# The recurrence of the last mixer: levels walked upwards in place, by products of gates

## What is computed

```python
f = lb + (1.0 - lb) * sigmoid(f_logit)
k = 1.0 - f
S_t = diag(f_t) S_(t-1) + k_t i_t^T          # 128 x 128 per head
o_t = S_t^T (q_t * 128 ** -0.5)
o = o * rsqrt(mean(o * o) + eps) * norm_g * silu(gate)
```

## Time and profile before

| | us |
|---|---|
| median of three executions | 3402.69 |
| the profiled execution | 3395.66 |
| its span, first to last instruction | 3393.8 |
| TensorE busy in the span | 3285.3 |
| recurrence, from 2340 to 2437 | 97 |

### The profile page before, as it was taken

How to read it: one execution, slowest core, us unless ns; L and a number is a source line. 1 busy time by engine, 2 the same in 40 slices (tenths; PEclk the granted TensorE clock), 3 DMA queues, 4 the chain that set the end, 5 groups by cost and what they waited for, 6 DMA issues and landing times.

```text
span 3393.8 us, 48243 instructions
## 1 busy us (share of the span) xinstructions
PE 3285.3 (97%) x16266; PEld 2647.4 (78%) x16266; DVE 1973.4 (58%) x2513; ACT 1761.5 (52%) x2142; POOL 1335.6 (39%) x670
## 2 busy tenths in 40 slices
PE   8999999999999999999999999998899999999997
PEld 6888887778888788888778888787666788888884
DVE  4335684653354433551563333457766799999998
ACT  5552334545523555322545533414662688888884
POOL 3444442144444444444134444343202344444441
PEclk9999999999999999999999999899999999999998
DMA  3225331022243222433422233222102899999997
GB/s 125 97 95 168 117 102 50 20 88 98 98 160 130 82 99 93 158 127 118 131 75 94 98 95 104 68 97 93 38 8 73 324 384 384 388 387 390 381 370 294
DMA packets 128099, 534.40 MB, mean 157 GB/s; under 512 B 24464, under 2 KB 24720, under 8 KB 100112
## 3 DMA queue, kind: packets, MB, share of 16 engines
q1 hardware_dynamic: 107136, 499.63, 41.5%
q0 software_dynamic: 20736, 33.60, 2.6%
q10 hardware_dynamic: 144, 0.08, 0.0%
HBM read 531.64 MB, written 41.94 MB: 169 GB/s over the span
## 4 chain that ended last, share of the span: by engine, by line
PE 60%; issue 25%; POOL 8%; DVE 5%; ACT 2%; DMA 1%; POOLq 0%; DVEq 0%; SPq 0%; ACTq 0%
PE ps L827 17%; PE ps L829 16%; PE ps L828 16%; POOL w_lo L1927 8%; PE ps L1308 2%; PE ps L989 1%; PE ps L1014 1%; PE ps L999 1%; PE ps L1373 1%; PE ps L847 1%; PE ps L1060 1%; PE ps L1129 1%; PE ps L1093 1%; PE ps L1292 0%; PE ps L1327 0%
## 5 line engine op out<-in xcount | busy, mean ns | idle before, releaser
L1927 POOL TENSOR_TENSOR w_lo<-stage_buf,w_hi 128x1024 fp32r<-128x1024 f32 (+1 forms) x396 | 968.9, 2447 | 1508.6 <-ACT w_hi L1471 1508.6
L1471 ACT ACTIVATE w_hi<-stage_buf 128x1024 fp32r<-128x1024 f32 (+1 forms) x396 | 414.0, 1046 | 1186.9 <-PE ps L829 1126.1
L827 PE MATMUL ps<-x_hi,w_hi 128*128 128x512 f32 x1984 | 776.1, 391 | 7.3 <-POOL w_lo L1927 5.6
L828 PE MATMUL ps<-x_lo,w_hi 128*128 128x512 f32 x1984 | 774.7, 390 | 0.0
L829 PE MATMUL ps<-x_hi,w_lo 128*128 128x512 f32 x1984 | 774.5, 390 | 0.0
L827 PE MATMUL ps<-hid,w_hi 128*128 128x512 f32 x1312 | 518.8, 395 | 2.6 <-issue 1.7
L829 PE MATMUL ps<-hid,w_lo 128*128 128x512 f32 x1312 | 511.6, 390 | 0.0
L828 PE MATMUL ps<-hid,w_hi 128*128 128x512 f32 x1312 | 510.8, 389 | 0.0
L827 PEld LDWEIGHTS ps<-x_hi,w_hi 128*128 128x128 f32 x1984 | 374.2, 189 | 89.3 <-POOL w_lo L1927 7.5
L829 PEld LDWEIGHTS ps<-x_hi,w_lo 128*128 128x128 f32 x1984 | 374.0, 189 | 77.6
L828 PEld LDWEIGHTS ps<-x_lo,w_hi 128*128 128x128 f32 x1984 | 374.2, 189 | 77.3
(11 more groups left out here) (405 smaller groups left out, 4952.8 us busy)
## 6 DMA issues: line engine op xcount, KB each, us to landing
stage_buf<-in_gu SPq DMA_DIRECT2D x176, 512.0 KB, 3.3
big<-in_exp_gu SPq DMA_DIRECT2D x72, 1024.0 KB
h_buf<-in_exp_gu SPq DMA_DIRECT2D x72, 1024.0 KB
s_buf<-in_exp_dn SPq DMA_DIRECT2D x72, 1024.0 KB
stage_buf<-in_down SPq DMA_DIRECT2D x64, 512.0 KB, 3.6
stage_buf<-in_down SPq DMA_DIRECT2D x32, 384.0 KB, 3.2
sil_buf<-in_ada SPq DMA_DIRECT2D x24, 512.0 KB, 4.3
tmp_buf<-in_ada SPq DMA_DIRECT2D x24, 512.0 KB, 4.2
```

The lines of the kernel that those rows point to most:

```text
L827: nc.tensor.matmul(o, a_hi, b_hi, start=start, stop=False)
L828: nc.tensor.matmul(o, a_hi, b_lo, start=False, stop=False)
L1471: nc.scalar.activation(w_hi[s][:, 0:n], stage[s][:, 0:n], ACT.Copy).then_inc(upper_done, 1)
L1927: nc.gpsimd.tensor_tensor(w_lo[s][:, 0:n], stage[s][:, 0:n], w_hi[s][:, 0:n].bitcast(F32), ALU.subtract).then_inc(parted, 1)
```

## The change

The tree is walked upwards, from neighbours to halves of a block, and no logarithm is taken. `hgrn_decays` multiplies neighbouring gates once, pairs of those again, and so on, which gives the decay of each run of 2, 4, ... 128 tokens (`hg_decay`). Query and key tiles (`hg_qw`, `hg_kw`) hold all four heads and are updated in place: before level r, whose halves are `1 << (r - 1)` wide, they are what its scores need; after it the queries of the second halves are multiplied with the decay of the first half and the keys of the first halves with that of the second (one factor, repeated over the run). Level 0 is the diagonal, with the raw queries. Heads are done in pairs: step i is level `i % 16 // 2` of head `i // 16 * 2 + i % 2`. Levels 6 and 7 compute only the pieces they need. What crosses blocks uses the same tiles once more: `near` (next block), one more update of one block, and `far`; ScalarE makes these copies now. Head sums and the rows of heads 2 and 3 are placed later, partly inside `gated`. The diff, cut, eight columns of indentation taken off:

```diff
-hg_b = [rstd[:, :]] + [xn_buf[:, (4 + hd) * T:(5 + hd) * T] for hd in range(1, 4)]
-hg_e = [tmp[:, 0, :], tmp[:, 1, :], s_buf[:, 5 * T:6 * T], s_buf[:, 6 * T:7 * T]]
-hg_kl, hg_ql = ([s_buf[:, (j + s) * T:(j + s + 1) * T] for s in range(2)] for j in (0, 2))
+hg_qw, hg_kw = tiles(s_buf[:, 0:4 * T], T), tiles(pt_buf[:, 0:4 * T], T)
+hg_scores = [tiles(s_buf[:, (4 + hd) * T:(5 + hd) * T], P) for hd in range(4)]
+hg_decay = [big[:, R_HF:R_HG], tmp_buf[:, :]] + [sil_buf[:, 1024 - (1024 >> n):1024 - (512 >> n)] for n in range(6)]
+hg_far = [xn_buf[:, 768 * j:768 * j + 768] for j in range(2)]
...
-hg_scores = [b[:, 4 * T:5 * T] for b in (s_buf, pt_buf)]
-X_PAIRS = [(a, b) for a in range(TT) for b in range(a + 1, TT)]
+def hg_bank(i):
+    return i % 2 if i >= 16 else 4 + i % 2
+def hg_at(r, hd):
+    return 16 * (hd // 2) + 2 * (r - 1) + hd % 2 + 1
+def hg_step(i):
+    return i % 16 // 2, i // 16 * 2 + i % 2
+def hg_halves(tile, half):
+    x = tile.rearrange("p (n c) -> p n c", c=2 * half)
+    return x[:, :, 0:half], x[:, :, half:2 * half]
+def hg_decays(r, hd):
+    n = T >> (r - 1)
+    x = hg_decay[r - 1][:, n * hd:n * hd + n].rearrange("p (n c) -> p n c", c=2)
+    shape = [P, n // 2, 1 << (r - 1)]
+    return x[:, :, 0:1].to_broadcast(shape), x[:, :, 1:2].to_broadcast(shape)
...
+    def head_sum(hd):
+        pe.wait_ge(hg["o_sq"], hd + 1)
+        if hd == 0:
+            pe.wait_ge(cm["step"], 1)
+        else:
+            pe.wait_ge(hg["o_std"], hd)
...
+    def head_rows(hd):
+        pe.wait_ge(factor, FACTOR_AT[f"head{hd}"] + 1)
+        if hd in (1, 2):
+            pe.wait_ge(hg["o_out"], hd)
+        token_rows(7 if hd == 3 else 6, hg_inv[hd]).then_inc(factor, 1)
...
             if i == 0:
+                head_sum(3)
+                head_rows(2)
                 pe.wait_ge(hg["o_std"], 4)
+                pe.wait_ge(hg["o_out"], 3)
...
             if i == 2:
-                pe.wait_ge(factor, FACTOR_AT["head3"] + 1)
                 pe.wait_ge(att["c_less"], 1)
-                token_rows(7).then_inc(factor, 1)
+                head_rows(3)
...
+        def bank_waits(i):
+            if i == 0:
+                pe.wait_ge(evac_done, u("tok_2") + 2 + CHUNKS["tok_2"][0]["units"])
+            elif i == 16:
+                pe.wait_ge(evac_done, u("tok_2") + 2 + 8)
+            elif i % 16 >= 2:
+                r, hd = hg_step(i - 2)
+                if r < 6:
+                    pe.wait_ge(hg["mul"], 12 * (hd // 2) + 2 * r + hd % 2 + 1)
+                else:
+                    pe.wait_ge(hg["rect"], 4 * (hd // 2) + 2 * (r - 6) + hd % 2 + 1)
+        def scores(i):
+            r, hd = hg_step(i)
+            bank_waits(i)
+            pe.wait_ge(hg["decay"], 2 if r == 0 else 3)
+            if r >= 2:
+                pe.wait_ge(hg["q"], hg_at(r - 1, hd))
+                pe.wait_ge(hg["k"], hg_at(r - 1, hd))
+            o = ps[:, hg_bank(i), :]
+            for t in range(TT):
+                if r < 6:
+                    c = slice(t * P, t * P + P)
+                    last = nc.tensor.matmul(o[:, c], hg_kw[:, hd, c], (hg_qw if r else q)[:, hd, c], start=True, stop=True)
+                else:
+                    half = 1 << (r - 1)
+                    for a in range(0, P, 2 * half):
+                        ks, qs = (slice(t * P + a + d, t * P + a + d + half) for d in (0, half))
+                        last = nc.tensor.matmul(o[a:a + half, qs], hg_kw[:, hd, ks], hg_qw[:, hd, qs], start=True, stop=True)
+            last.then_inc(hg["qk"], 1)
+        def near(hd):
+            pe.wait_ge(hg["q"], hg_at(7, hd))
+            pe.wait_ge(hg["k"], hg_at(7, hd))
+            if hd == 0:
+                pe.wait_ge(evac_done, u("tok_2") + 2 + 8)
+            elif hd == 2:
+                pe.wait_ge(hg["x_sb"], 2)
+            for n, a in enumerate((0, 2)):
+                c = 256 * (hd % 2) + n * P
+                last = nc.tensor.matmul(ps[:, 3, c:c + P], hg_kw[:, hd, a * P:a * P + P], hg_qw[:, hd, a * P + P:a * P + 2 * P],
+                                        start=True, stop=True)
+            last.then_inc(hg["x_near"], 1)
+        def far(hd):
+            pe.wait_ge(hg["q"], hg_at(8, hd))
+            pe.wait_ge(hg["k"], hg_at(8, hd))
+            if hd == 3:
+                pe.wait_ge(hg["rect"], 7)
+            elif hd >= 1:
+                pe.wait_ge(hg["x_sb"], hd + 2)
+            for a in range(2):
+                last = nc.tensor.matmul(ps[:, 0 if hd == 3 else 2, 256 * a:256 * a + 256], hg_kw[:, hd, a * P:a * P + P],
+                                        hg_qw[:, hd, 256:512], start=True, stop=True)
+            last.then_inc(hg["x_far"], 1)
         def values(hd):
-            pe.wait_ge(hg["mul"], 6 * (hd + 1))
+            pe.wait_ge(hg["mul"], 12 * (hd // 2) + 10 + hd % 2 + 1)
+            pe.wait_ge(hg["rect"], 4 * (hd // 2) + 2 + hd % 2 + 1)
+            if hd >= 2:
+                pe.wait_ge(hg["o_out"], hd - 1)
             for b in range(TT):
-                last = nc.tensor.matmul(ps[:, 4 + hd % 2, b * P:b * P + P], v[:, b, hd * P:hd * P + P],
-                                        tiles(hg_scores[hd % 2], P)[:, b, :], start=False, stop=(b == TT - 1))
+                nc.tensor.matmul(ps[:, 4 + hd % 2, b * P:b * P + P], v[:, b, hd * P:hd * P + P], hg_scores[hd][:, b, :],
+                                 start=(b == 0), stop=False)
+        def far_values(hd):
+            pe.wait_ge(hg["x_sb"], 4 * (hd // 2) + 3 + hd % 2)
+            for a, (c, w) in enumerate(((0, 384), (384, 256), (640, 128))):
+                last = nc.tensor.matmul(ps[:, 4 + hd % 2, T - w:T], v[:, a, hd * P:hd * P + P], hg_far[hd % 2][:, c:c + w],
+                                        start=False, stop=(a == 2))
             last.then_inc(hg["pv"], 1)
...
+        for i in range(32):
+            scores(i)
             if i < 16:
                 compress_step(2 * i)
                 compress_step(2 * i + 1)
-            if i == 20:
+            elif i == 16:
+                near(0)
+            elif i == 17:
+                near(1)
+            elif i == 18:
+                values(0)
+            elif i == 19:
+                far(0)
+            elif i == 20:
+                values(1)
+            elif i == 21:
+                far_values(0)
+            elif i == 22:
+                far(1)
+            elif i == 23:
+                head_sum(0)
+            elif i == 24:
+                far_values(1)
+            elif i == 25:
+                head_rows(0)
+            elif i == 26:
+                head_sum(1)
+            elif i == 27:
                 turn_compressed()
...
+            elif i == 28:
+                head_rows(1)
+        near(2)
+        near(3)
+        values(2)
+        far(2)
+        values(3)
+        far(3)
+        compressed_heads()
+        far_values(2)
+        far_values(3)
+        head_sum(2)
...
     def hgrn():
-        def head_norm(hd):
+        def rectangles(p):
+            for i in range(16 * p + 12, 16 * p + 16):
+                r, hd = hg_step(i)
+                half = 1 << (r - 1)
+                act.wait_ge(hg["qk"], i + 1)
+                act.wait_ge(hg["mul"], 12 * p + 10 + hd % 2 + 1)
+                for a in range(0, P, 2 * half):
+                    nc_in = tiles(ps[:, hg_bank(i), :], P)[a:a + half, :, a + half:a + 2 * half]
+                    last = nc.scalar.activation(hg_scores[hd][a:a + half, :, a + half:a + 2 * half], nc_in, ACT.Copy)
+                last.then_inc(hg["rect"], 1)
...
+        rectangles(0)
+        near(0)
+        near(1)
+        far(0)
+        squares(0)
+        far(1)
+        roots(0)
+        squares(1)
+        roots(1)
+        sigmoids()
+        root_table()
+        rectangles(1)
+        near(2)
+        near(3)
+        far(2)
+        far(3)
+        squares(2)
+        squares(3)
+        roots(2)
...
-            weights("tok_2", hook=hgrn_log)
+            weights("tok_2")
             hgrn()
-            for j in range(2):
-                upper("out_2", 0, 2, j)
+            upper("out_2", 0, 2, 0)
+            roots(3)
+            upper("out_2", 0, 2, 1)
...
+        def key(r, hd):
+            first, _ = hg_halves(hg_kw[:, hd, :], 1 << (r - 1))
+            if r > 1:
+                pool.wait_ge(hg["k"], hg_at(r - 1, hd))
+            nc.gpsimd.tensor_tensor(first, first, hg_decays(r, hd)[1], ALU.mult).then_inc(hg["k"], 1)
+        def last_key(hd):
+            pool.wait_ge(hg["x_near"], hd + 1)
+            pool.wait_ge(hg["k"], hg_at(7, hd))
+            c = hg_kw[:, hd, 0:P]
+            nc.gpsimd.tensor_scalar(c, c, hg_decay[7][:, TT * hd + 1:TT * hd + 2], None, ALU.mult).then_inc(hg["k"], 1)
+        pool.wait_ge(hg["decay"], 10)
+        for i in range(32):
+            r, hd = hg_step(i)
+            if r == 0:
+                continue
+            if i == 18:
+                last_key(0)
+                last_key(1)
+            pool.wait_ge(hg["qk"], i + 1)
```

(82 more changed lines are left out.)

220 lines of the change are left out of this document (26 added, 194 removed).

## The result

The changed kernel takes 3378.77 us (median of 6 runs, 3370.75 to 3382.14), the kernel before, timed beside it, 3401.76 (3393.45 to 3403.03): 23.0 us faster, ratio 0.9934, 95% interval 0.9919 to 0.9948. Timed twice more beside the kernel before, the changed kernel stood at 3376.45 against 3396.87 and at 3378.09 against 3396.53, so 20.4 and 18.4 faster: the 23.0 is the largest of three.

A forecast was written before the change was run, and what follows sets the result against it. No engine was full in the 97 us recurrence; handing work round between engines set its length. Attention 12.2 us earlier less 1.2 lost inside it gave 11.0, so 3391.7 us, range 3381 to 3404.

The forecast's parts named there:

- Part 1: Start of the stage: logarithm gone, products of 2048 down to 16 columns replace scans; steady work starts at 2342.9.
- Part 2: Steps 0 to 15: TensorE needs 2.1 us a step; 31.0 plus 1.7 for the clock, ending at 2375.6.
- Part 3: Steps 16 to 25, no compress work left: TensorE bounds with 19.4 us, to 2395.0.
- Part 4: Steps 25 to 29: VectorE's list takes 11.8 us, GELU ends at g = 2406.8; TensorE gap of some 6.
- Part 5: Tail behind the GELU: 3.2, then 9.35 in series on TensorE, 3.0 for the clock; attention 12.2 earlier.
- Part 6: Work moved into the attention: 2.7 us later, 1.5 gained by faster compressed scores, net 1.2 lost.
- Rival 1: Tail without hole: GELU 3 us sooner, clock loses 0 to 1, compressed scores fast; gain 17, 3385.7; chance 0.17.
- Rival 2: Tail: all 9.35 us run at 1.2 GHz, compressed scores slow as before; gain 3.5, 3399.2; chance 0.22.
- Rival 3: GpSimd's key with a repeated factor takes 2.5 us, deciding from 2.0; 12 slower, 3415; chance 0.08.
- Rival 4: Steps 0 to 25: VectorE always loses the port and bounds; gain 8.5, 3394.2; chance within the forecast's 0.50.

The follow-up runs named there:

- experiment 8: Changed kernel with scores of levels 6 and 7 computed as whole 128x128 tiles instead of only their pieces; 3374.05 us in one run.
- load experiment: Changed kernel with one extra useless product of 512 columns on VectorE in each of the 32 steps; 3388.14 us in one run.
- early GELU: Changed kernel with transposes and GELU moved to steps 20 and 21, sigmoid ahead of ScalarE's first square root; 3372.54 us, ratio 0.9932; again 3372.68.
- filled hole: Changed kernel with twenty useless 128-column matmuls on TensorE between steps 29 and 30; 3376.28 us, ratio 0.9948.
- late head: The early GELU kernel with its memsets in step 4 and head 1's output behind the last queries; 3372.05 us, ratio 0.9928; again 3374.26.
- head by head: Changed kernel without interleaving: each head of a pair goes through all eight levels before the other; 3386.71 us, ratio 0.9973.

## Why the prediction was right in its direction and too low in its size

| term | forecast | measured |
|---|---|---|
| gates to first compress matmul | 32.07 | 32.13 |
| steps 0 to 15 | 32.7 | 31.5 |
| steps 16 to 25 | 19.4 | 16.9 |
| steps 25 to 29, to the end of the GELU | 11.8 | 10.0 |
| GELU to scores 30 | 2.0 | 2.1 |
| scores 30 to the near groups' end | 3.2 | 4.0 |
| from there to the attention | 9.35 | 8.2 |
| added for the clock in the tail | 3.0 | in the two above |
| lost by the part moved into the attention | 1.2 | 2.1 |

The forecast's gain was 11.0, the measured one at the same point 18.7, and the differences add up: 1.1 + 2.5 + 1.8 + 3.2 - 0.9 = 7.7. The attention won back 1.1 more, to 19.8 at the end of the span. The remaining 3.2 of the timed 23.0 are in no stage of these traces; the later timings, 20.4 and 18.4, lie about the traced value. By the traced gain alone the time would have been near 3383, inside the range: the terms below were wrong by 7.7, and what carried the time over the edge of the range is a difference that no trace holds.

*Part 1* was right to 0.1 in its sum, the links included (a link is an engine's wait for its own last instruction). It was partly luck: the first product took 2.59, not 2.28, and the small ones and links less than their terms. *Part 2* was right: compress matmuls at 2346.24, then pairs 2.09 apart, no gap but 0.27 at 2375.41; only the four small steps were cheaper (the 32-column group at 2371.84 is followed 0.37 later, not 0.9; the 64-column one at 2376.32 0.46 later, not 0.55). The 1.7 for the clock at the start was 1.55 by the comparison in experiment 8. The load experiment bears out that VectorE and GpSimd are hidden there.

*Part 3 is the first step that failed*, by its size. It took "10 score groups at 1.0 (two groups take 1.95)". The row of sixteen matmuls in the earlier trace rows is 1.95 long, but the lengths of successive rows overlap, and from start to start one group is 0.89. On all the groups of this part that is 2.5 us. Its reading, TensorE bounds and nothing waits, was right.

*Part 4* had the mechanism: the GELU holds ScalarE, ScalarE holds the bank, and TensorE stands for 5.63 ("some 6"), from step 30 at g + 2.08 ("g + 2.0"). The early GELU removed just this gap. The list of VectorE was 1.8 shorter than the sum. In part its rows overlap in the same way: the next instruction starts up to 0.1 before the length of the one before is over (2400.92 0.69, then 2401.53). Another 0.5 is the GELU, 2.64 instead of 3.2, whose first product took 0.96 before and 0.42 now, and one of the two reciprocals was already done at 2393.64. The rest I did not separate.

*Part 5 is the second that failed*, by the size of its clock term. Three microseconds were charged for a low stretch of six; by the filled hole it was 1.15. The stretch at 0.50 had been taken from a place where TensorE was busy throughout, and 9.35 for the list again used row lengths (8.2 by the starts). With the 3.2 ahead of it the tail was charged 15.6 and took 12.3.

*Part 6*: the moved work cost 3.1 ahead of the 64 small matmuls instead of 2.7 (3.64 against 0.55 from the attention's start, the wait of 0.94 included). The hope that they would run at full speed came true for 2.0 us only: then the clock fell, and they took 5.0 from start to start against 5.4. The premise was loose as well: before, the clock was at 1.00 for the first 1.4 us of the 64, and the earlier trace rows shows the 0.50 only beside the sixteen behind them.

```profile
2422.00:2425.00 3.00, 2.32 (x39) 2.35 (x40) 1.02 (x6) 2.93 (x9) 3.00 (x2) 0.94 0.34 100
2425.00:2428.00 3.00, 3.00 (x30) 3.00 (x31) 0.00 (x0) 0.00 (x0) 0.11 (x1) 0.50 0.74 254
```

*The rivals.* Rival 1 came nearest with its number (a gain of 17; 18.7 at this mark), and two of its three conditions came true, the GELU sooner (5.4, not 3) and the clock costing about 1; but the hole was there, so its title was wrong, and the compressed scores weren't fast. That it came near is partly luck. Rival 2 is refuted by the filled hole: 1.15 where it needed 6. Rival 3, the slow key, is refuted: keys took 0.62 to 1.09, against a deciding point of 2.0. Rival 4, the port always lost, is refuted: in 23 of the 28 pairs VectorE starts 0.03 to 0.11 us ahead of the key and its query takes 0.41 to 0.43. Four queries start 0.01 to 0.28 behind a key and take 0.62 to 0.95; one starts 0.51 behind, when the key is nearly over, and takes 0.42. VectorE and GpSimd rows, one pair of each kind:

```profile
2383.41 0.43 DVE L2619 TENSOR_TENSOR s_buf<-s_buf,big 128x256 f32<-128x256 f32 x1 [0.69 <-PE ps L1174]
...
2385.27 0.95 DVE L2619 TENSOR_TENSOR s_buf<-s_buf,tmp_buf 128x256 f32<-128x256 f32 x1 [0.21 <-PE ps L1174]
```

```profile
2383.45 1.09 POOL L2049 TENSOR_TENSOR pt_buf<-pt_buf,big 128x256 f32<-128x256 f32 x1 [0.69 <-PE ps L1174]
2385.21 0.74 POOL L2049 TENSOR_TENSOR pt_buf<-pt_buf,tmp_buf 128x256 f32<-128x256 f32 x1 [0.67 <-PE ps L1174]
```

Where VectorE starts 0.04 ahead (0.43 long), the key takes 1.09; where it comes 0.06 later, it takes 0.95 and the key 0.74. In the seventh experiment, where queries are held up, their mean rises from 473 to 638 ns and that of the keys falls from 827 to 732. The Trainium skill, "SBUF — State Buffer", Terms, speaks of one shared port pair held to the end of an instruction; these rows agree.

## What to carry to other kernels

Sum a list of matmul groups by the distance of their starts, never by the length column: here that alone was 15% of a term. Where a ring of four engines sets the pace, putting two independent rings side by side pays most where nothing else covers the wait; the same interleaving was worth 2.2 us beside dense work and up to 6.4 without it. Before trusting a difference of one or two microseconds between two profiles, look whether the clock fell at the same places in both. Look at what an engine with a long list still has to do near the end of a stage: a burst with no hurry, set before the one copy that frees a bank, cost more than the clock it brought down.

## What the runs showed of the hardware that was not expected

- The clock fell inside the gap of 5.6 us and stayed at its 1.2 GHz level until about 2411, but the net price was only 1.15 us.
- The length of a gap doesn't tell whether the clock falls. Before, it stayed at 1.00 through the gap of 3.22 us ahead of 2412.53; behind the wait of 2.7 us ahead of the first compress matmul it fell in ten of the eleven profiles of the changed code, and in the eighth experiment it did not.
- The 64 small attention matmuls of 32 columns take 3.9 to 6.7 us from start to start in kernels that differ only ahead of them. All start at the 1.00 clock behind the same wait of 0.94 us, and in all the clock falls to 0.50 while they run; their time follows from when: 3.3 us after their start, 3.9 in all (early GELU); 2.0 after, 5.0 (changed kernel); 0.8 after, 6.1 (late head); 0.15 after, 6.7 (head by head). What decides that moment was not tried.
- A GpSimd product whose second operand is one element repeated over 1 to 64 columns costs no more than a plain one (0.62 to 1.09 us for 256 columns a partition, 0.72 to 1.28).
